# Where VectorE makes the seventh slab's lower part in the first turn of two feed-forwards

## The reference, cut to what matters

```
def modulate(h, shift, scale):
    return h * (1.0 + scale) + shift

def swiglu(h, w_in, w_out):
    gate, up = jnp.split(h @ w_in, 2, axis=-1)
    return (jax.nn.silu(gate) * up) @ w_out
```

## Time and profile before

| | |
|---|---|
| Median of three runs | 2528.65 us (2527.76 to 2529.94) |
| The profiled execution's own time | 2527.66 us |
| Its span | 2525.9 us |
| TensorE, VectorE, ScalarE, GpSimd busy | 96%, 66%, 42%, 15% |
| Mean granted TensorE clock | 0.992 |

### The profile page before, as it was taken

The page is one execution under the profiler, slowest core; times in us unless marked ns, Lnnn a source line. Parts: engine busy times, 40 slices in busy tenths (PEclk is TensorE's granted clock), DMA queues, the critical chain, the costliest instruction groups (busy, mean ns, idle before and its releaser), DMA issues.

```text
span 2525.9 us, 46179 instructions
## 1 busy us (share of the span) xinstructions
PE 2424.0 (96%) x17946; PEld 1974.5 (78%) x17946; DVE 1673.5 (66%) x2767; ACT 1056.4 (42%) x1746; POOL 376.2 (15%) x342
## 2 busy tenths in 40 slices
PE   7999999989898999999999999999999999999998
PEld 4888888857776788888788888769998885677877
DVE  3777787666565787778887763775556324665665
ACT  4222224365444632222522223565446234655354
POOL 2000001022353200000100001001012800211052
PEclk9999999999999999999999999999999999999999
DMA  7655663200000365566465553214563231013311
GB/s 291 220 195 194 194 202 114 90 30 3 4 4 20 115 215 193 191 195 199 164 200 191 194 154 101 94 62 159 182 177 120 92 100 63 18 43 125 114 46 51
DMA packets 88422, 323.35 MB, mean 128 GB/s; under 512 B 9712, under 2 KB 10864, under 8 KB 87504
## 3 DMA queue, kind: packets, MB, share of 16 engines
q1 hardware_dynamic: 86864, 310.68, 38.0%
q0 software_dynamic: 1408, 10.59, 1.1%
HBM read 320.18 MB, written 1.05 MB: 127 GB/s over the span
## 4 chain that ended last, share of the span: by engine, by line
PE 83%; DVE 7%; issue 4%; ACT 3%; DMA 1%; DVEq 1%; POOLq 0%; POOL 0%; ACTq 0%; SPq 0%
PE bank L503 23%; PE bank L505 22%; PE bank L504 22%; PE bank L1406 1%; DMA weight_ring<-stream_k 1%; PE bank L2270 1%; PE bank L1435 1%; PE bank L1417 1%; DVE row_statistics L1464 1%; DVE weights_hi_lo L409 1%; PE bank L2276 1%; PE bank L1840 1%; ACT weights_hi_lo L404 1%; PE bank L3262 1%; PE bank L2328 1%
## 5 line engine op out<-in xcount | busy, mean ns | idle before, releaser
L404 ACT ACTIVATE weights_hi_lo<-weight_ring 128x1024 fp32r<-128x1024 f32 (+1 forms) x379 | 394.6, 1041 | 1079.2 <-PE bank L505 1053.1
L503 PE MATMUL bank<-input_hi,weights_hi_lo 128*128 128x512 f32 (+1 forms) x2032 | 742.9, 366 | 15.1 <-DVE weights_hi_lo L409 9.1
L504 PE MATMUL bank<-input_lo,weights_hi_lo 128*128 128x512 f32 (+1 forms) x2032 | 739.5, 364 | 0.0
L505 PE MATMUL bank<-input_hi,weights_hi_lo 128*128 128x512 f32 (+1 forms) x2032 | 739.2, 364 | 0.0
L409 DVE TENSOR_TENSOR weights_hi_lo<-weight_ring,weights_hi_lo 128x1024 fp32r<-128x1024 f32 (+1 forms) x373 | 453.1, 1215 | 427.3 <-ACT weights_hi_lo L404 425.6
L503 PEld LDWEIGHTS bank<-input_hi,weights_hi_lo 128*128 128x128 f32 x2032 | 385.5, 190 | 82.0 <-issue 19.0
L504 PEld LDWEIGHTS bank<-input_lo,weights_hi_lo 128*128 128x128 f32 x2032 | 385.6, 190 | 60.4 <-issue 0.7
L505 PEld LDWEIGHTS bank<-input_hi,weights_hi_lo 128*128 128x128 f32 x2032 | 385.4, 190 | 59.8
L503 PE MATMUL bank<-hidden_hi_lo,weights_hi_lo 128*128 128x512 f32 (+1 forms) x936 | 335.9, 359 | 4.5 <-DVE weights_hi_lo L409 4.1
L505 PE MATMUL bank<-hidden_hi_lo,weights_hi_lo 128*128 128x512 f32 (+1 forms) x936 | 333.6, 356 | 0.0
L504 PE MATMUL bank<-hidden_hi_lo,weights_hi_lo 128*128 128x512 f32 (+1 forms) x936 | 333.6, 356 | 0.0
(11 more groups left out here) (531 smaller groups left out, 2940.3 us busy)
## 6 DMA issues: line engine op xcount, KB each, us to landing
weight_ring<-stream_k SPq DMA_DIRECT2D x498, 512.0 KB, 3.5
weight_ring<-stream_f SPq DMA_DIRECT2D x64, 448.0 KB, 3.5
weight_ring<-stream_f SPq DMA_DIRECT2D x32, 512.0 KB, 3.7
extra_tiles<-condrows POOLq DMA_DIRECT2D x3, 1024.0 KB, 9.1
constants<-consts POOLq DMA_DIRECT2D x1, 2112.5 KB, 9.3
residual_stream<-xin SPq DMA_DIRECT2D x1, 2048.0 KB, 11.0
work<-nabias POOLq DMA_DIRECT2D x1, 2048.0 KB, 9.2
residual_stream<-ctx POOLq DMA_DIRECT2D x1, 1024.0 KB, 5.8
```

Source lines behind the costliest of these rows:

```text
L404: act.activation(split_place(place)[:, 0, 0:words], w[:, 0:words], ACT.Copy).then_inc(hi_ready, 1)
L503: pe.matmul(out, weights[:, 0, w], x_hi, start=first, stop=False)
L504: pe.matmul(out, weights[:, 0, w], x_lo, start=False, stop=False)
L505: return pe.matmul(out, weights[:, 1, w], x_hi, start=False, stop=last)
```

## The change

In the first turn of the second and third feed-forward VectorE makes the lower part of the seventh slab behind the third modulation slab and in front of the fourth, in place of behind the placing of the four. In every other turn but the last, of all four feed-forwards, the lower part that stood at the head of the next turn stands at the end of this one, behind the placing. The instructions are the same, with the same waits.

```diff
@@ -1282,6 +1282,10 @@
             slabs, s0, s1 = out_slabs(f), SPLIT_AT[f"ffn_in{f}"][0], SPLIT_AT[f"ffn_out{f}"][0]
             n0, p1 = SLAB_AT[f"ffn{f}"][0], DONE_AT[f"ffn_out{f}"][0]
 
+            def split_next(i, n, t, each):
+
+                split_lo(dve, 0, n + 4 * each + 2, counted(i, s0 + 2 * t + 7, 4))
+
             def turn(i, n, p, t, each, first, last):
                 for k in range(4):
                     j = k // 2
@@ -1292,7 +1296,7 @@
                         dve.tensor_tensor(HIDDEN[:, j, a:b], GATE[:, a:b], pb[k][:, a:b], ALU.mult).then_inc(hidden, 1)
                     if last and k >= 2:
                         split_lo(dve, k, slabs[k - 2][0], s1 + k - 1, slabs[k - 2][1])
-                    elif not first or k > (FFN_NORMS[f] in RAW_NORMS):
+                    elif k > (FFN_NORMS[f] in RAW_NORMS if first else 0):
                         split_lo(dve, k, n + each * k + 2, counted(i, s0 + 2 * t + k + 3, 4))
                     if k % 2:
                         dve.wait_ge(hidden_hi, counted(i, f * FT + t + j + 1, 2))
@@ -1301,10 +1305,15 @@
                     if mods_beside(f):
                         if first and k == (2 if f else 0):
                             dve.wait_ge(cond_ready, f + 1)
-                        for q in (((), (), (0, 1), (2, 3))[k] if first and f else (k,)):
+                        for q in (((), (), (0, 1), (2,))[k] if first and f else (k,)):
                             mod_product(dve, n + 2 * q + 3, q, i, 8)
+                if first and f and mods_beside(f):
+                    split_next(i, n, t, each)
+                    mod_product(dve, n + 9, 3, i, 8)
                 if mods_beside(f):
                     mod_place(dve, MOD_BATCHES[FFN_BATCHES[f]][0] + 2 * t, i)
+                if not last and not (first and f and mods_beside(f)):
+                    split_next(i, n, t, each)
 
             ffn_loop(dve, f, turn)
             lo, hi = MOD_BATCHES[FFN_BATCHES[f] + 1] if mods_beside(f) else (0, 0)
```

## The result

| | before | changed |
|---|---|---|
| Median | 2529.98 us (2525.93 to 2533.82, 20 runs) | 2532.92 us (2527.78 to 2538.77, 20 runs) |
| Ratio to before | | 1.0013, 95% interval 1.0007 to 1.0019 |
| The profiled execution's own time | 2527.66 us | 2536.52 us |
| Its span | 2525.9 us | 2534.7 us |

The wait that the change removes in front of the seventh slab comes back in front of the eighth, and the kernel gets no faster. The change costs 3.3 us by the ratio (1.8 to 4.8 by its interval); the medians lie 2.9 us apart. Twice more the same kernel was timed beside before, 11 runs each: 1.0004 (0.9995 to 1.0013) both times. The three ratios, weighted by the inverse square of their intervals, give 1.0009 (1.0004 to 1.0013), some 2.2 us.

A forecast was written before the change was run, and what follows sets the result against it. TensorE, busy 96% of the span, was taken as the bound, with VectorE what it waits for next; +0.11 and +0.20 us at the eighth slab, +0.3 on 2528.65, gave 2529.0 us, range 2526.8 to 2530.8.

The forecast's parts named there:

- VectorE's idle time: Before the seventh slab's lower part, second feed-forward: VectorE stands 0.97 us for ScalarE's upper part, 886.42 to 887.39.
- the 7.5 us from one subtraction to the next: VectorE, first turn: from the seventh slab's lower part to the eighth's, 7.51 us forecast.
- the step from the placing to the fifth product: VectorE, into the second turn: not shown by the trace, taken as 0.35 us, bounds 0.24 and 0.51.
- the ninth slab's load: Issued 1.1 us later, with 1.1 us left, costing nothing; rival: lands over 7.4 us after issue, about 2531, chance 0.05.
- the free edge of the loops: Subtraction at a turn's end: an edge of a few tenths is hidden by 2.8 us of TensorE's work.
- upper part at 1250.81 + 1.06 = 1251.87: Third feed-forward, seventh slab: upper part ready then, so the eighth slab starts +0.20 us later, between +0.09 and +0.36.
- whose issue the diff leaves alone: Load behind the seventh slab's upper part: issue unchanged, so the upper part comes no earlier; ScalarE idled 3.45 us for it.
- the order on VectorE stays in all other turns: All other turns of all four feed-forwards: only the loop's edge moves, behind the subtraction; nothing added to the sum.
- The eighth slab not late: Rival, both first turns: the 1.45 us stay gained, some 3.1 us with the pipeline's restart, giving 2525.5; chance 0.07.
- The 0.97 us not lost: Rival, VectorE at the seventh slab: out of order or earlier upper part, 1.5 us shorter, 2527.2; chance 0.03.
- No effect: Rival: the wait before the seventh slab stays, only if its upper part came 1.9 us later; 2528.65, chance 0.02.
- The loop's edge: Rival, 27 loop turns: an edge over 2.8 us longer costs each turn the excess; 0.2 us excess gives 2534; chance 0.03.

The follow-up runs named there:

- order_only: Kernel before with the seventh slab's lower part ahead of the fourth modulation slab in both first turns, second turn written out, loops untouched; 1.0004 (0.9995 to 1.0013).
- before_early_load: Kernel before, with the seventh slab's load issued early; 1.0000 (0.9990 to 1.0009) of the kernel before.
- early_load: Changed kernel, with the seventh slab's load issued right behind the fifth slab's subtraction; 1.0000 (0.9991 to 1.0009) of the kernel before.
- pad_as_change: Kernel before, order untouched, with one more VectorE drain per feed-forward to give later instructions the change's numbers; 1.0003 (0.9994 to 1.0012).
- after_again: The changed kernel, unaltered, timed and profiled a second time; 1.0004 (0.9995 to 1.0013) of the kernel before.

## Why the prediction was wrong

**What held.** TensorE waited for VectorE and nothing else; the wait in front of the seventh slab went and came back in front of the eighth; VectorE's idle time (0.88 us measured, 0.97 forecast), the 7.5 us from one subtraction to the next, the step from the placing to the fifth product (0.37 us measured, 0.35 taken), the ninth slab's load (issued 1.2 us later, no wait) and the free edge of the loops came out as written. The order alone is worth nothing (order_only; the second feed-forward of each profile of the change).

**The step that failed first** is the third feed-forward's, "upper part at 1250.81 + 1.06 = 1251.87", +0.20 us with +0.36 as its bound. In the three profiles the eighth slab started 0.76, 0.55 and 0.45 us later, and with its first matmul behind a wait the stretch was 0.89, 0.70 and 0.62 us longer. The upper part was late by 0.7, 0.5 and 0.4 us. I took the load's landing as given, a load "whose issue the diff leaves alone". The diff did leave the issue alone, and moved a fetch of VectorE's instructions within the transfer, from 10.9 us behind the silu to about 10. And I priced the ninth slab's load but not this one, on which the new order has no cover: in the old one 1.87 us lay between the end of the upper part (887.36) and the start of the subtraction at 889.23, and 1.74 us in the third feed-forward. An earlier load brings nothing there (before_early_load) and 0.9 us in each place in the new one (early_load).

**The step that was missing** is what one more instruction per feed-forward does to all that follows on VectorE. That the order on VectorE stays in all other turns was true, and was no reason to cost the rest at nothing: the odd mixer, 430 us behind the third feed-forward's first turn, stopped for 0.43 us in a place where TensorE waited. From 1681 to 1730 us that went with 0.78, 0.49 and 0.77 us in the change's profiles and 0.73 in pad_as_change (0.3 for the stop; but for after_again 0.95 for the clock and 0.5 back). The 0.3 is shown to be the stop's; the clock's part is not.

Together 1.2 to 1.7 us are accounted for, profile by profile, against 3.3 (1.8 to 4.8) in the first timing and 2.2 (1.1 to 3.3) over three. What is left lies within the interval of the three; of the first timing it leaves a little over. Whether something else is in it stays open.

**The range** also stood on too few runs. Three runs gave before 2528.65; twenty gave 2529.98. Of the 3.9 us by which 2529.0 missed, 1.3 are this. The spread of the three was taken for the runs' spread, and the runs lie 8 to 11 us apart.

**The rivals.** The eighth slab not late: no. The 0.97 us not lost: no, VectorE stood for 0.88; that the fourth modulation product did not go ahead doesn't tell the order of VectorE's queue from the drain that stands in front of the product. No effect: no, the wait moved. The ninth slab's load: no. The loop's edge: it cost nothing inside the loops and 0.2 us at each entry behind the placing (7.46 against 7.26 us), but it brought the extra instruction. The slower side did not come from any of them.

## What to carry to other kernels

Where one engine is behind by more work than the wait is long, moving a subtraction ahead moves the wait by one slab. Here only taking work out of the stretch, or spreading it over two turns with spare time, took most of it away. Before calling a load harmless ask what covered its landing in the old order. A rearrangement that changes the number of instructions of an engine, even by one, can move short stops hundreds of microseconds away; count to where the blocks of its program end. Differences under 2 us of a 2.5 ms kernel then need not be the reordered stretch's: one profile of a kernel differed by 3.7 us from another in a stretch of 100, and only short stretches compared between several profiles tell them apart.

## What the runs showed of the hardware

Packets of 8 KB of the instruction queue q14 go with VectorE's program. A packet 2.5 to 2.8 us behind the issue of a load of 512 KB went with an upper part at 12.4 to 12.7 us behind the silu in five profiles; with the packet ahead of the issue, 3.5 us or more behind it, or absent, it was 11.7 to 12.0 in six. VectorE's stops of about 0.43 us (0.37 to 0.47) all lie at one place in each block of 128 instructions of its program, 107 times in 18 traces. What it stops for the traces don't name; in the odd mixer the packet goes out behind the stop. The Trainium skill ("Advanced Engine Details and Errata", ISA Cache) has instructions in cache lines of 16 KB, 256 instructions each; the trace agrees that instructions come in blocks, and its packets on this queue are of 8 KB, its blocks of 128.
